# Two attentions of a three-layer network on one core: copies ahead of exponentials, a mask that changes engines, one transfer moved up

## The reference, cut to what matters

```python
def forgetting_attention(q, k, v, f_pre):            # 8 heads of 64
    F = jnp.cumsum(jax.nn.log_sigmoid(f_pre), axis=-1)
    ...
        logits = einsum('bhqd,bhkd->bhqk', qb, k) * scale + fq[..., :, None] - F[..., None, :]
        logits = jnp.where(kpos[None, :] <= qpos[:, None], logits, -jnp.inf)
        p = jax.nn.softmax(logits, axis=-1)
        return einsum('bhqk,bhkd->bhqd', p, v)

def dsa_sparse_attention(q, k, v, iq, ik, iw):       # 8 heads of 128, 2 key heads
        rel = jax.nn.relu(einsum("bqhd,bsd->bqhs", iq_b, ik))
        score = einsum("bqh,bqhs->bqs", iw_b, rel)
        score = jnp.where(causal[None], score, -jnp.inf)
        _, idx = lax.top_k(score, k_top)             # 128 keys a query
        ...
        p = jax.nn.softmax(logits, axis=-1)          # over the chosen keys
        o = jnp.einsum("bqgrk,bqkgd->bqgrd", p, v_sel)
```

## Time and profile before

| | |
|---|---|
| median of 3 runs | 2177.53 us (2177.52 to 2177.66) |
| the profiled execution, its own time | 2177.74 us |
| its span, first to last instruction | 2176.0 us |
| TensorE busy | 2135.4 us, 98% |
| VectorE busy | 1285.1 us, 59% |
| ScalarE busy | 917.7 us, 42% |
| DMA queue of SyncE | 28.1% of 16 engines |
| fox attention, TensorE's part | about 179 to 249 us |
| sparse attention, TensorE's part | 1396.04 to 1467.43 us |

### The profile page before, as it was taken

How to read it: one execution, slowest core, us unless ns; L and a number is a source line. 1 busy time by engine, 2 the same in 40 slices (tenths; PEclk the granted TensorE clock), 3 DMA queues, 4 the chain that set the end, 5 groups by cost and what they waited for, 6 DMA issues and landing times.

```text
span 2176.0 us, 26697 instructions
## 1 busy us (share of the span) xinstructions
PE 2135.4 (98%) x10620; PEld 1730.3 (80%) x10620; DVE 1285.1 (59%) x1966; ACT 917.7 (42%) x1550; POOL 101.5 (5%) x155
## 2 busy tenths in 40 slices
PE   9999999999999999999999999999999999999998
PEld 7866688888888658888888878777788878888887
DVE  6446475555347767655543749456677657555634
ACT  4235553334325456333432642344445545333421
POOL 0000040000000003100000000000012200000000
PEclk9999999999999999999999999999999999999999
DMA  5312123333323203333332323202222023333332
GB/s 201 97 59 78 60 96 97 97 97 116 97 78 107 68 30 126 97 97 97 116 97 88 126 78 90 75 30 87 79 77 68 2 78 98 97 97 98 117 97 77
DMA packets 51099, 194.00 MB, mean 89 GB/s; under 512 B 5665, under 2 KB 5665, under 8 KB 49953
## 3 DMA queue, kind: packets, MB, share of 16 engines
q1 hardware_dynamic: 50976, 192.30, 28.1%
HBM read 188.09 MB, written 4.19 MB: 88 GB/s over the span
## 4 chain that ended last, share of the span: by engine, by line
PE 88%; DVE 5%; ACT 5%; issue 1%; DMA 1%; SPq 0%; ACTq 0%; DVEq 0%
PE bank L403 26%; PE bank L404 26%; PE bank L405 26%; PE bank L980 2%; PE bank L703 1%; DMA ring<-stream 1%; ACT arena L1265 1%; PE bank L681 1%; DVE small L1889 1%; ACT whi L1160 1%; PE bank L618 1%; DVE arena L2010 0%; DVE xs L1884 0%; PE bank L692 0%; PE bank L775 0%
## 5 line engine op out<-in xcount | busy, mean ns | idle before, releaser
L403 PE MATMUL bank<-xs,whi 128*128 128x512 f32 (+2 forms) x1992 | 770.8, 387 | 8.4 <-DVE xs L1884 2.9
L405 PE MATMUL bank<-xs,wlo 128*128 128x512 f32 (+2 forms) x1992 | 750.1, 377 | 0.0
L404 PE MATMUL bank<-xs,whi 128*128 128x512 f32 (+2 forms) x1992 | 749.9, 376 | 0.0
L1863 DVE TENSOR_TENSOR wlo<-ring,whi 128x1024 fp32r<-128x1024 f32 x333 | 415.2, 1248 | 294.8 <-ACT whi L1160 294.3
L1160 ACT ACTIVATE whi<-ring 128x1024 fp32r<-128x1024 f32 x333 | 350.4, 1054 | 262.4 <-DMA ring<-stream 262.2
L403 PEld LDWEIGHTS bank<-xs,whi 128*128 128x128 f32 x1992 | 375.4, 188 | 93.4 <-issue 12.2
L405 PEld LDWEIGHTS bank<-xs,wlo 128*128 128x128 f32 x1992 | 375.2, 188 | 69.0
L404 PEld LDWEIGHTS bank<-xs,whi 128*128 128x128 f32 x1992 | 375.8, 189 | 67.2 <-issue 2.9
L403 PE MATMUL bank<-whi,xs 128*128 128x512 f32 (+1 forms) x808 | 314.8, 390 | 1.6 <-issue 0.9
L405 PE MATMUL bank<-whi,xs 128*128 128x512 f32 (+1 forms) x808 | 311.7, 386 | 0.0
L404 PE MATMUL bank<-wlo,xs 128*128 128x512 f32 (+1 forms) x808 | 311.6, 386 | 0.0
(11 more groups left out here) (367 smaller groups left out, 1781.3 us busy)
## 6 DMA issues: line engine op xcount, KB each, us to landing
ring<-stream SPq DMA_DIRECT2D x333, 512.0 KB, 3.6
arena<-gains SPq DMA_DIRECT2D x5, 1024.0 KB, 5.8
arena<-xt SPq DMA_DIRECT2D x4, 512.0 KB, 6.1
arena<-xn SPq DMA_DIRECT2D x1, 2048.0 KB, 8.0
kept<-arena SPq DMA_DIRECT2D x1, 2048.0 KB, 7.2
arena<-kept SPq DMA_DIRECT2D x1, 2048.0 KB, 8.0
out<-arena SPq DMA_DIRECT2D x3, 512.0 KB, 2.6
con<-consts SPq DMA_DIRECT2D x1, 744.0 KB, 11.6
```

The costliest lines, as they stand in the source:

```text
L403: nc.tensor.matmul(out, ah, bh, start=first, stop=False)
L404: nc.tensor.matmul(out, ah, bl, start=False, stop=False)
L405: return nc.tensor.matmul(out, al, bh, start=False, stop=last)
L1863: V.tensor_tensor(wlo[:, v % SLOTS, :], ring[:, v % SLOTS, :], whi[:, v % SLOTS, :], ALU.subtract).then_inc(wlo_done, 1)
```

## The change

Four things are changed; what is computed stays the same up to rounding.

1. **Start.** SyncE issues unit 1 ahead of the parameters.
2. **Fox attention, ScalarE.** In each round the copies (L1323 of finished sums, L1329 of turned probabilities) come ahead of the exponential.
3. **Sparse attention, order.** ScalarE's copy of turned probabilities comes ahead of the exponential too. Transposes go from two rounds behind the logits to three, value products from three to four, VectorE's multiplication by finished sums from four to five. The weight splits go from round 1 of eight to round 5.
4. **Sparse attention, mask.** The 32 mask products are gone from TensorE. VectorE's maximum becomes `tensor_tensor_reduce`, which forms -(logits + mask), writes it back over the logits in PSUM, and takes the minimum of it in the same pass. The exponential reads it with scale -1. The wait for the masks goes from TensorE's round 1 to VectorE's.

```diff
@@ SyncE @@
+            sp.dma_start(ring[:, 1, :], stream[1]).then_inc(ring_sem[1], 16)
             sp.dma_start(par[:], params).then_inc(par_sem, 16)
-            for s in (1, 2, 3):
+            for s in (2, 3):
@@ the steps of dsa @@
-                          more=[(idb[:], madd[:, i, 0:(i + 1) * P] if i else mqb[:], 0, (i + 1) * P)],
+                          mask=madd[:, i, 0:(i + 1) * P] if i else mqb[:],
@@ TensorE, attention() @@
-                        if n == 1:
-                            pe.wait_ge(vector_out, vector_at.find("masks"))
-                        nc.tensor.matmul(bank[b][:, 0:W], st["q"], st["k"], start=True, stop=False)
-                        for x, (l, r, c0, c1) in enumerate(st["more"]):
-                            m = nc.tensor.matmul(bank[b][:, c0:c1], l, r, start=False, stop=x == len(st["more"]) - 1)
-                        m.then_inc(tensor_out, tensor_at.next(name, "logits", n))
+                        nc.tensor.matmul(bank[b][:, 0:W], st["q"], st["k"], start=True, stop=True).then_inc(...)
...
-                    if 2 <= n < N + 2:
-                        k, st = n - 2, steps[n - 2]
+                    if 3 <= n < N + 3:
+                        k, st = n - 3, steps[n - 3]
...
-                    if n >= 3:
-                        k, st = n - 3, steps[n - 3]
+                    if n >= 4:
+                        k, st = n - 4, steps[n - 4]
@@ ScalarE, attention() @@
+                    if 3 <= n < N + 3:
+                        ... the copy of step n - 3 ...
                     if n < N:
...
-                        A(st["ps"][:, 0:W], bank[st["lb"]][:, 0:W], ACT.Exp, bias=small[:, 200 + n % 4:201 + n % 4],
+                        A(st["ps"][:, 0:W], bank[st["lb"]][:, 0:W], ACT.Exp, bias=small[:, 200 + n % 4:201 + n % 4], scale=-1.0,
...
-                    if 2 <= n < N + 2:
-                        ... the copy of step n - 2 ...
@@ ScalarE, paired_attention(): the block of the exponential moved behind the two copies @@
@@ ScalarE and VectorE, between_heads() @@
-                    if x == 1 and j < COUNT["z2b"]:
+                    if x == 5 and j < COUNT["z2b"]:
@@ VectorE, attention() @@
-                    if name == "dsa" and n >= 4 and steps[n - 4]["last"]:
+                    if name == "dsa" and n >= 5 and steps[n - 5]["last"]:
...
-                        V.tensor_reduce(small[:, 200 + n % 4:201 + n % 4], bank[...][:, 0:steps[n]["w"]], AX_X, ALU.max, negate=True).then_inc(...)
+                        logits, top = bank[steps[n]["lb"]][:, 0:steps[n]["w"]], small[:, 200 + n % 4:201 + n % 4]
+                        if name == "dsa":
+                            if n == 1:
+                                dve.wait_ge(vector_out, vector_at.find("masks"))
+                            V.tensor_tensor_reduce(logits, logits, steps[n]["mask"], -1.0, 3e38, ALU.add, ALU.min, top).then_inc(...)
+                        else:
+                            V.tensor_reduce(top, logits, AX_X, ALU.max, negate=True).then_inc(...)
```

More of the change, by code:

```diff
@@ L673, in attention @@
                 N = len(steps)
-                for n in range(N + 3):
+                for n in range(N + 4):
                     if n < N:
@@ L678, in attention @@
                         W = st["w"]
[L679 to L684 removed]
+                        nc.tensor.matmul(bank[b][:, 0:W], st["q"], st["k"], start=True, stop=True).then_inc(tensor_out, tensor_at.next(name, "logits", n))
                         reader[b] = (SCALAR, (name, "exp", n))
[L686 to L687 removed]
+                    if 3 <= n < N + 3:
+                        k, st = n - 3, steps[n - 3]
                         b = 5 + k % 2
@@ L1289, in attention @@
                 N = len(steps)
-                for n in range(N + 3):
+                for n in range(N + 4):
                     if ahead is not None:
                         ahead(n)
+                    if 3 <= n < N + 3:
+                        k, st = n - 3, steps[n - 3]
+                        act.wait_ge(tensor_out, tensor_at.find(name, "t", k))
+                        if k >= 3:
+                            act.wait_ge(tensor_out, tensor_at.find(name, "pv", k - 3))
+                        A(st["ts"][:, 0:st["w"]], bank[5 + k % 2][:, 0:st["w"]], ACT.Copy).then_inc(scalar_out, scalar_at.next(name, "pt", k))
                     if n < N:
```

28 lines of the change are left out of this document (12 added, 16 removed).

## The result

The changed kernel takes 2159.99 us in the median of 4 runs (2157.87 to 2161.47), the kernel before 2177.53 beside it. The ratio is 0.9919, 95% interval 0.9902 to 0.9936. The profiled execution of the changed kernel took 2160.94 us, its span is 2159.2. One run of a kernel further down (c2) took 4313.86 us, twice its other three, and is left out of every comparison.

The account below looks back on a forecast made before the run. TensorE, busy for 98% of the span, was taken as the bound. Terms 1.2 + 2.5 + 4.6 + 4.6 = 12.9 us off 2177.74 gave 2164.8, less 0.2 for the median: 2164.6 us, range 2161.8 to 2168.

Parts of the forecast that it names:

- plays no part: Start, fox and sparse attention: clock column 1.00, full 2.4 GHz on both sides of the change, so no term for it.
- The fox attention, 3.2 - 0.7 = 2.5 us: Fox attention: five TensorE waits for ScalarE's copies go, 3.2 us, less 0.7 for later waits; bounds 0 and 3.9.
- The start, 1.2 us: Start: unit 1 no longer waits behind the parameters' transfer, gain 1.2 us; bounds 0.9 and 1.6.
- The masks, 4.6 us: Sparse attention: 32 mask products leave TensorE, gain 4.6 us from start to start; bounds 3.6 and 4.8.
- The waits of the sparse attention, 4.6 us: Sparse attention: TensorE's waits go through later transposes, early copy and moved splits, gain 4.6 us; bounds 2.5 and 5.9.
- The maximum's price: Sparse attention, VectorE: the new operation costs what the plain maximum does, 0.688 us at 512 columns.
- The 4.9 us for reads: Sparse attention, VectorE: 32 second instructions at 0.153 us add 4.9 us to its busy time, costing the kernel nothing.
- A: Sparse attention: new operation costs what the scan does, VectorE at its limit, repeated waits stay; 2167.3 us; chance 0.13.
- B: Fox attention: the new ScalarE order gives nothing, waits only change names; 2167.1 us; chance 0.12.
- C: Sparse attention: a fixed cost of VectorE's new operation makes the kernel slower, 2195.5 us at 1.8 us each; chance 0.04.
- D: All touched stretches: every term reaches its upper bound, 16.2 us gained, 2161.3 us; chance 0.10.
- fed as before: Behind each touched stretch: TensorE's weight units arrive as before, so no gain comes back as a later wait.

Follow-up runs that it names:

- c2: Changed kernel with masks back on TensorE and weight splits back in round 1, leaving only the new order in the sparse attention: 2164.91 us, ratio 0.9946.
- d1: Changed kernel unedited, run again beside other kernels on one chip: 2161.74 us, ratio 0.9929.
- b2: Kernel before with only the sparse attention's masks moved to VectorE, old order kept: 2174.22 us, ratio 0.9987.
- a1: Kernel before with only unit 1 issued ahead of the parameters at the start: 2176.22 us, ratio 0.9996.
- a2: Kernel before with only ScalarE's order in the fox attention changed, exponential behind both copies: 2173.02 us, ratio 0.9984.

## Why the prediction was wrong

- **The clock "plays no part".** This step failed. I read the clock column of the touched stretches, all 1.00, and took it for the whole. Elsewhere before has 17 us at 1.2 GHz in four stretches of its profiled execution (6.83 and three of 3.41), the changed kernel 14 in three; they vary from run to run and cost a quarter to half of their length. Of the 4.6 us by which the forecast missed, 17.5 - 15.1 = 2.4 lie outside the traced stretches, and by the table of equal clocks most of them go with this; so does nearly all the spread of the runs. The range had no term for it: the 15.1 us of the stretches alone would have given 2162.4, inside the range. The other 2.2 us are the terms below that came out larger, the fox attention (1.2) and the waits of the sparse attention (1.1) above all. That the four runs of the first comparison had a mean clock 0.001 above before's is in part luck of the draw: the five of d1 had none of it.
- **The fox attention, 3.2 - 0.7 = 2.5 us.** The mechanism is right, the size off: measured 3.7, near the upper bound of 3.9. What failed is the window of the sum, not its discount. The waits were counted from 220 us on the earlier trace rows, and there the term was nearly right: between 220 and 250 us the lead grows by 2.6 (2.38 to 4.99; with the fox order alone 1.24 to 3.86). The gate's wait at 226 took back 0.2 of the 0.3 allowed, and one of the last two waits stayed, the one for the copy of sums at 244 us (0.3). The other 1.0 us was won ahead of 220, which the sum left out: 0.2 near 189 us, 0.5 from 190 to 194, where from the value products to the product that waits for the gate it was 1.41 us before (192.70 to 194.11) and is 1.07 now (190.96 to 192.03), and 0.3 near 209. That the chain had four rounds of cover held.
- **The start, 1.2 us.** Measured 1.3 (1.2 in the mean of 13 traces), with a gap of 0.5 against the 0.4 expected and the high half at 11.40.
- **The masks, 4.6 us.** Measured 4.4 with the new order. A mask of 128 columns was priced at 0.09 a slot, and part of that was the transposes' wait: the one at 1403.95 us takes 0.06.
- **The waits of the sparse attention, 4.6 us.** Measured 10.1 - 4.4 = 5.7, under the upper bound of 5.9. This term is 1.1 us too small. Only the total is measured; no run prices the single waits. In the trace before TensorE stops in the drain from 1463.77 to 1464.20, 0.4 us, which I had kept for the upper bound; the other 0.7 are not placed.
- **VectorE.** The maximum's price was right: 697 ns at 512 columns against 688. The rule weighed in the forecast, half throughput for two SBUF sources that aren't bf16 (the Trainium skill, "Vector Engine (DVE) Microarchitecture Reference", section 7), doesn't bind one PSUM and one bf16 source, and the trace agrees with that: the operation takes 9 ns more than the maximum, not twice as long. The 4.9 us for reads were wrong as load on VectorE: they lie beside other work. Rivals A, B and C are out: A and C by the added maxima, B by the fox order alone. D, 2161.3 by upper bounds, was nearest; its fox term (3.9) and its waits (5.9) nearly came true, its start and masks did not, and the rest of the way to 2160.0 was the clock, so that it was nearest by luck in part.
- **Weight units "fed as before".** Near enough: TensorE's wait for a low half near 1788 us, 0.90 us over the usual spacing in the trace before, is smaller in every other trace, and the leads change there by 0.3 to 1.0 us.

## What to carry to other kernels

Price each stop that a change ends from start to start, and over the whole stretch: here the fox sum was nearly right from 220 us on and missed the 1.0 us ahead of it. Where TensorE is nearly always busy, look in the trace for stretches at the lower clock outside the edited code as well; the runs spread with them, and kernels are best compared at equal clock or stretch by stretch. A removed piece of work is worth its time only where the order can use it: masks off TensorE gave 2.0 us alone and 4.4 with transposes a round later and the splits moved.

## What the runs showed of the hardware

- An add with a running minimum over 128x512, PSUM and bf16 SBUF in, PSUM out, took 697 ns, a plain maximum 688; its accumulator read of 142 ns starts with the next instruction and costs nothing.
- A stop of TensorE of 5.2 us was followed by 3.41 us at 1.2 GHz; stops of 1.47 and 0.65 us with short work between them by 6.83 us; one of 1.69 us (before) and one of 1.92 (b2) by none, those of 1.90 and 1.91 (a1, a2) by 3.41 us, which began over 1 us after work had gone on.
- A lower stretch can go on under full work. The d1 kernel, TensorE busy for 10.10 of 10.24 us:

```profile
1653.21:1663.45 10.24, 10.10 (x63) 9.45 (x63) 2.35 (x5) 5.15 (x15) 8.71 (x29) 0.50 0.01 2
```
